# Low parts of some weight units made by GpSimd instead of VectorE, in a two-layer hybrid decoder on one Trainium2 core

## What is computed

```python
for l in range(DEPTH):                       # 2
    h = _rmsnorm(x, ln_g[l])                 # x: (1, 256, 2048) float32
    u = h @ w_in[l]                          # w_in: (2048, 6232)
    ...                                      # y_a GLA, y_b SSD, y_c MLA, y_d dilated attention
    y = jnp.concatenate([y_a, y_b, y_c, y_d], axis=-1)
    x = x + y @ w_out[l]                     # w_out: (2048, 2048)
```

## Time and profile before

| | us |
|---|---|
| median of 3 runs | 840.86 (840.15 to 841.04) |
| profiled execution | 841.09 |
| its span | 839.3 |
| PE busy | 833.8 |
| DVE busy | 525.9 |
| ACT busy | 475.0 |
| POOL busy | 47.1 |

### The profile page before, as it was taken

How to read it: one execution, slowest core, us unless ns; L and a number is a source line. 1 busy time by engine, 2 the same in 40 slices (tenths; PEclk the granted TensorE clock), 3 DMA queues, 4 the chain that set the end, 5 groups by cost and what they waited for, 6 DMA issues and landing times.

```text
span 839.3 us, 11336 instructions
## 1 busy us (share of the span) xinstructions
PE 833.8 (99%) x4350; PEld 703.4 (84%) x4350; DVE 525.9 (63%) x872; ACT 475.0 (57%) x788; POOL 47.1 (6%) x63
## 2 busy tenths in 40 slices
PE   9999999999999999999999999999999999999998
PEld 6888888997888888888888888889888888888886
DVE  6566764774886565644564577638749865556542
ACT  7666544776865566443546564456677565663441
POOL 7200000100200000000000000001002000000000
PEclk9999999999999999999999999999999999999999
DMA  9976652564654445656656666526546544546663
GB/s 342 336 252 215 210 174 82 170 169 131 182 174 150 151 134 167 200 186 193 205 191 189 187 217 193 176 82 192 143 124 202 169 148 128 176 132 215 195 188 123
DMA packets 46165, 150.97 MB, mean 180 GB/s; under 512 B 5344, under 2 KB 6032, under 8 KB 45600
## 3 DMA queue, kind: packets, MB, share of 16 engines
q1 hardware_dynamic: 45168, 147.62, 55.6%
q10 hardware_dynamic: 752, 2.57, 0.9%
q0 software_dynamic: 192, 0.07, 0.0%
HBM read 148.13 MB, written 2.11 MB: 179 GB/s over the span
## 4 chain that ended last, share of the span: by engine, by line
PE 97%; DVE 1%; ACT 1%; issue 0%; DMA 0%; ACTq 0%; DVEq 0%
PE gemm L637 28%; PE gemm L646 27%; PE gemm L638 27%; PE pairs L828 2%; PE pairs L714 1%; PE pairs L854 1%; PE pairs L843 1%; PE pairs L668 1%; PE pairs L835 1%; PE pairs L799 1%; PE pairs L568 1%; PE pairs L869 1%; DVE u L1483 0%; PE pairs L881 0%; PE pairs L882 0%; PE pairs L880 0%
## 5 line engine op out<-in xcount | busy, mean ns | idle before, releaser
L1359 DVE TENSOR_TENSOR w_lo<-raw,w_hi 128x1024 fp32r<-128x1024 f32 (+1 forms) x287 | 318.1, 1115 | 237.1 <-ACT w_hi L995 236.1
L637 PE MATMUL gemm<-w_hi,a_hi 128*128 128x512 f32 (+1 forms) x1144 | 425.2, 377 | 0.9 <-ACT w_hi L995 0.9
L638 PE MATMUL gemm<-w_hi,a_lo 128*128 128x512 f32 (+1 forms) x1144 | 414.3, 368 | 0.0
L995 ACT ACTIVATE w_hi<-raw 128x1024 fp32r<-128x1024 f32 (+1 forms) x287 | 273.9, 968 | 181.1 <-PE gemm L646 159.2
L646 PE MATMUL gemm<-w_lo,a_hi 128*128 128x512 f32 (+1 forms) x1144 | 281.4, 368 | 0.0
L637 PEld LDWEIGHTS gemm<-w_hi,a_hi 128*128 128x128 f32 x1144 | 215.1, 188 | 37.0 <-issue 2.6
L638 PEld LDWEIGHTS gemm<-w_hi,a_lo 128*128 128x128 f32 x1144 | 215.3, 188 | 33.6 <-issue 1.0
L646 PEld LDWEIGHTS gemm<-w_lo,a_hi 128*128 128x128 f32 x1144 | 203.6, 188 | 35.0
L1025 ACT ACTIVATE u<-gemm,st 128x512 f32<-128x512 f32 (+1 forms) x40 | 22.1, 604 | 15.9 <-PE gemm L646 15.9
L1209 ACT ACTIVATE arena<-arena,st 128x128 f32<-128x128 f32 (+1 forms) x32 | 13.1, 444 | 28.2 <-DVE st L1579 28.2
L542 POOL TENSOR_TENSOR st<-st,powers 128x4 f32<-128x4 f32 (+2 forms) x8 | 1.9, 240 | 446.6 <-ACT arena L1079 220.7
(11 more groups left out here) (197 smaller groups left out, 605.3 us busy)
## 6 DMA issues: line engine op xcount, KB each, us to landing
raw<-in_weights_dram SPq DMA_DIRECT2D x223, 512.0 KB, 3.6
raw<-in_weights_dram SPq DMA_DIRECT2D x64, 278.0 KB, 2.9
wuq<-in_w_uq_dram SPq DMA_DIRECT2D x2, 1152.0 KB, 6.1
x<-in_x_dram SPq DMA_DIRECT2D x4, 512.0 KB, 6.2
o<-ssd_rows ACTq DMA_DIRECT2D x2, 1024.0 KB, 6.6
param_rows<-in_params_dram SPq DMA_DIRECT2D x2, 904.0 KB, 7.6
u<-in_xT_dram SPq DMA_DIRECT2D x3, 512.0 KB, 8.1
out_dram<-x SPq DMA_DIRECT2D x3, 512.0 KB, 6.0
```

The lines of the kernel that those rows point to most:

```text
L637: pe.matmul(acc_t[t], a_hi[:, k, tok[t]], hi, start=k == 0, stop=False)
L638: pe.matmul(acc_t[t], a_lo[:, k, tok[t]], hi, start=False, stop=False)
L995: A_(w_hi[:, n % SPLIT, 0:c], raw[:, n % RAW, 0:c], ACT.Copy).then_inc(hi_done, 1)
L1359: TT(w_lo[:, n % SPLIT, 0:c], raw[:, n % RAW, 0:c], w_hi[:, n % SPLIT, 0:c].bitcast(F32), ALU.subtract).then_inc(split_done, 1)
```

## The change

From unit 12 of layer 0 on, and in all of layer 1, the low part of each unit with n % 4 == 3 is made by POOL, with the same subtraction on the same tiles; DVE skips these units. The one count `split_done` is replaced by two, `split["dve"]` and `split["pool"]`, and `split_of(l, n)` gives the count to wait for: how many units up to this one that engine has split. PE and SP wait for it; for its first four loads SP waits for nothing, and DVE no longer sets the count at the start. On POOL the eight reciprocal roots are placed between the subtractions by the table RSQRT_AT: a root stands behind the unit of its number, and behind that unit's subtraction if POOL has one there. It is 33 units in layer 0 and 36 in layer 1, 16 of them narrow.

```diff
--- before.py
+++ after.py
@@ -104,6 +104,10 @@
 WARM = 3
 
 GLA_AT = 26
+
+POOL_FROM = 12
+
+RSQRT_AT = {"x rs": 13, "gla rs": 47, "mla crs": 57, "mla rs 0": 74, "mla rs 1": 78, "dil rs 0": 81, "dil rs 1": 83, "ssd rs": 94}
 
 LEVELS = (64, 32, 16, 8, 4, 2, 1)
 NEG = -1e30
@@ -404,7 +408,8 @@
         row_out, row_in = sem("row_out"), sem("row_in")
         x_turned, x_hi, x_lo = sem("x_turned"), sem("x_hi"), sem("x_lo")
         weights_in = [sem(f"weights_in_{i}") for i in range(RAW)]
-        hi_done, split_done, unit_used = sem("hi_done"), sem("split_done"), sem("unit_used")
+        hi_done, unit_used = sem("hi_done"), sem("unit_used")
+        split = {"dve": sem("split_dve"), "pool": sem("split_pool")}
         stage = {e: sem(f"{e}_stages") for e in ORDER}
         setup = {e: sem(f"{e}_setup") for e in ORDER}
         seen = {e: [] for e in ORDER}
@@ -423,6 +428,15 @@
 
         def unit_width(n):
             return BLOCKS[n // UPB][2]
+
+        def splitter(l, n):
+
+            return "pool" if n % 4 == 3 and (l or n >= POOL_FROM) else "dve"
+
+        def split_of(l, n):
+
+            e = splitter(l, n)
+            return split[e], sum(splitter(*divmod(g, UNITS)) == e for g in range(l * UNITS + n + 1))
 
         def weights(l, n):
             return w_d[l, UNIT_AT[n]:UNIT_AT[n + 1]].rearrange("(p c) -> p c", p=P)
@@ -456,7 +470,8 @@
             for l in range(DEPTH):
                 for n in range(UNITS):
                     w = unit_width(n)
-                    sp.wait_ge(split_done, l * UNITS + n + 1)
+                    if l * UNITS + n >= RAW:
+                        sp.wait_ge(*split_of(*divmod(l * UNITS + n - RAW, UNITS)))
                     if (l, n) == (0, 0):
 
                         sp.dma_start(raw[:, 0, WB:2 * WB], weights(l, n)[:, WB:2 * WB]).then_inc(weights_in[0], 16)
@@ -547,14 +562,21 @@
 
                 pool.dma_start(w2[0:GLA_R, :], gla_w2[l]).then_inc(gate_in, 16)
                 pool.dma_start(w2[GLA_R:GLA_R + 1, :], gla_b[l].unsqueeze(0)).then_inc(gate_in, 16)
-                rsqrt("x rs", xrs, xss)
-                rsqrt("gla rs", grs, gss)
-                rsqrt("mla crs", crs, css)
-                rsqrt("mla rs 0", mrs[:, 0:8], mss[:, 0:8])
-                rsqrt("mla rs 1", mrs[:, 8:16], mss[:, 8:16])
-                rsqrt("dil rs 0", drs[:, 0:8], dss[:, 0:8])
-                rsqrt("dil rs 1", drs[:, 8:16], dss[:, 8:16])
-                rsqrt("ssd rs", brs, bss)
+                def lo(n):
+
+                    c = UK * unit_width(n)
+                    pool.wait_ge(hi_done, l * UNITS + n + 1)
+                    pool.tensor_tensor(w_lo[:, n % SPLIT, 0:c], raw[:, n % RAW, 0:c], w_hi[:, n % SPLIT, 0:c].bitcast(F32), ALU.subtract).then_inc(split["pool"], 1)
+
+                roots = {"x rs": (xrs, xss), "gla rs": (grs, gss), "mla crs": (crs, css), "mla rs 0": (mrs[:, 0:8], mss[:, 0:8]),
+                         "mla rs 1": (mrs[:, 8:16], mss[:, 8:16]), "dil rs 0": (drs[:, 0:8], dss[:, 0:8]),
+                         "dil rs 1": (drs[:, 8:16], dss[:, 8:16]), "ssd rs": (brs, bss)}
+                for n in range(UNITS):
+                    if splitter(l, n) == "pool":
+                        lo(n)
+                    for name, (dst, mean) in roots.items():
+                        if n == RSQRT_AT[name]:
+                            rsqrt(name, dst, mean)
 
                 pool.wait_ge(*reached("dve", l)("yT 3"))
 
@@ -600,7 +622,7 @@
                         pe.wait_ge(*dve(f"yT {(n - U_OUT) // 2}"))
                     if (l, n) == (DEPTH - 1, UNITS - 1):
 
-                        pe.wait_ge(split_done, l * UNITS + n + 1 + RAW)
+                        pe.wait_ge(*split_of(l, n))
                         for t in range(T):
                             acc_t, tok = acc_ps[:, b % 2, t, 0:w], slice(t * P, (t + 1) * P)
                             for j in range(UK):
@@ -623,7 +645,7 @@
                             for t in range(T):
                                 pe.matmul(acc_t[t], a_hi[:, k, tok[t]], hi, start=k == 0, stop=False)
                             if j:
-                                pe.wait_ge(split_done, 1 + RAW)
+                                pe.wait_ge(*split_of(0, 0))
                             else:
                                 pe.wait_ge(first_lo, 1)
                             pe.wait_ge(x_lo, j + 1)
@@ -1315,8 +1337,6 @@
         @block.vector
         def _(v):
             v.memset(A(0, WB), 0.0).then_inc(warm, 1)
-            v.sem_inc(split_done, RAW)
-
             v.wait_ge(cols_in, 16)
 
             def xT_lo(i, l):
@@ -1353,10 +1373,12 @@
                         xT_lo(0, 0)
                         xT_lo(1, 0)
                         v.wait_ge(hi_done, 1)
-                        TT(w_lo[:, 0, WB:c], raw[:, 0, WB:c], w_hi[:, 0, WB:c].bitcast(F32), ALU.subtract).then_inc(split_done, 1)
+                        TT(w_lo[:, 0, WB:c], raw[:, 0, WB:c], w_hi[:, 0, WB:c].bitcast(F32), ALU.subtract).then_inc(split["dve"], 1)
+                        return
+                    if splitter(l, n) == "pool":
                         return
                     v.wait_ge(hi_done, l * UNITS + n + 1)
-                    TT(w_lo[:, n % SPLIT, 0:c], raw[:, n % RAW, 0:c], w_hi[:, n % SPLIT, 0:c].bitcast(F32), ALU.subtract).then_inc(split_done, 1)
+                    TT(w_lo[:, n % SPLIT, 0:c], raw[:, n % RAW, 0:c], w_hi[:, n % SPLIT, 0:c].bitcast(F32), ALU.subtract).then_inc(split["dve"], 1)
 
                 def yT(j):
```

## The result

The changed kernel takes 842.35 us (median of 16 executions, 841.91 to 843.11), the kernel before 840.75 beside it. The ratio is 1.0019, 95% interval 1.0012 to 1.0027: 1.6 us slower, 1.0 to 2.3. It is a small loss, but the interval excludes no change. The profiled execution took 842.28 us, its span 840.4. POOL's subtraction is L569.

What follows compares the result with a forecast made beforehand. PE, busy 833.8 of 839.3 us, was taken as the bound, with at most 0.9 us to win. Layer 0's +0.6 and layer 1's +0.1 made +0.7 us: predicted median 841.5 us, range 840.1 to 843.4.

Steps and rivals of the forecast that it cites:

- The bound: Whole kernel: PE is busy 833.8 of 839.3 us, so the change can win at most 0.9 us.
- The price on POOL: POOL's subtractions, scaled from 0.60 us for 256 elements: 2.40 us for 1024 elements and 1.30 for 556.
- The lock: POOL and DVE block each other: POOL waits for DVE's running instruction, DVE's next waits for all of POOL's.
- The wide units: The 53 wide subtractions: about 8.9 us of slack for 2.4; tightest is unit 15 of layer 0. Cost 0.
- Step 1: Narrow stretch: POOL's subtraction for unit 51 blocks DVE's backlog, L1390 and the high part of 55 +0.5 us.
- Step 2: Unit 55's low part: POOL brings it 1.30 us behind the high part, PE wants it at 1.13: +0.15.
- Step 3, the loads: Unit 59's load goes some 1.1 us later, its high part comes 0.8 late, within cover: cost 0.
- Layer 1: Narrow stretch of layer 1: steps repeat at +0.6 us, idle time before unit 61 takes most: +0.1.
- the rival of blocking elsewhere: DVE's blocking reaches PE at attention steps or a root used by DVE: up to 1.2 us each, chance 0.05.
- The sum: Whole kernel: +0.6 us in layer 0 and +0.1 in layer 1 make +0.7, predicted median 841.5 us.
- Reciprocal roots between subtractions, the start, the end: POOL's eight roots queued between subtractions, SP's first four loads, and unit 143 of layer 1: cost 0 each.

Runs made afterwards that it cites:

- The best kernel here: Only the wide subtractions on POOL and ACT's silus one unit later, against the kernel before: 839.65 us, ratio 0.9988.

## Why the prediction was right or wrong, point by point

- **The bound: right.** PE's idle time between start and tail, 0.9 us, was taken as all that could be won. The best kernel here has none of it left and is 1.0 us faster (0.3 to 1.8).
- **The price on POOL: right for the wide ones, 7% low for the narrow.** 2.40 was forecast and 2.40 measured in most of the 53 (2469 ns in the mean, since some wait for DVE). For 556 elements I took 1.30 and it is 1.39 where nothing blocks it (unit 55). The two give (2.40 - 1.39)/468 = 2.2 ns an element and 0.2 us fixed, so neither strict proportion nor the 0.26 us row with its slope of 1.4 ns was right: the 0.60 that I read behind DVE's end already held little of the fixed part. The estimate from the figure of the Trainium skill, "GPSIMD Engine Reference", section "Performance versus the Vector engine" (2.25 and 1.22 us) was 6% and 12% low.
- **The lock: right.** A subtraction on POOL holds up DVE's two-operand instructions, and a memset doesn't.
- **The wide units: right.** No wait, ratio 0.9999 without the narrow ones. At unit 15 the cover left was to be 0.44 us and is 0.42 in the changed kernel.
- **Step 1: right in place and size.** +0.5 forecast, +0.47 and +0.41 measured. The idle time before unit 55 was to be 0.7 and is 0.64.
- **Step 2: right in place, too small.** +0.15 forecast, +0.44 in each layer. 0.09 is POOL's 1.39 for 1.30. For the rest the traces show two terms that the sum left out: PE's first matmul behind a wait is recorded at 0.39 us instead of 0.29, and POOL starts 0.08 us behind the end of the high part (164.73 to 164.81).
- **Step 3, the loads: right at a cost of 0, wrong in size.** No wait at 59 or 60. The high part of 59 was to be 0.8 us late. Against PE's schedule before the stretch it was 1.3 us late in layer 0 and 0.8 early in layer 1. Loads that nothing in the edit touches move as much (next point).
- **Layer 1: +0.1 forecast, +0.46 measured.** Unit 61 gave back 0.89 where I had 0.5. Missing was the low part of unit 62: I priced POOL's blocking where DVE's result reaches PE through ACT, and passed over a DVE w_lo with 0.54 us of cover right beside a subtraction on POOL. It was in the rival of blocking elsewhere, which named other places.
- **Unit 61's idle time hangs on the load of unit 59.** In layer 1 before, SP issues that load at 580.94 and ACT starts on it at 586.32, 5.4 us later. With unit 63 alone on POOL, where nothing of this layer differs up to there and the load is issued at the same point of PE's schedule, it is 581.63 and 585.86, 4.2 us, and PE isn't idle before unit 61. In both the chain from there (DVE's low part of 59, its last convolution step, ACT's silu, a table load) brings the high part of 61 some 4.6 to 4.7 us behind that of 59. These are ACT's rows with unit 63 alone and with the wide subtractions alone:

```profile
585.86 1.45 ACT L1017 ACTIVATE w_hi<-raw 128x556 fp32r<-128x556 f32 x2 [0.93 <-DMA raw<-in_weights_dram]
590.56 1.78 ACT L1017 ACTIVATE w_hi<-raw 128x556 fp32r<-128x556 f32 x3
...
585.59 1.40 ACT L1017 ACTIVATE w_hi<-raw 128x556 fp32r<-128x556 f32 x2 [1.27 <-DMA raw<-in_weights_dram]
590.24 1.79 ACT L1017 ACTIVATE w_hi<-raw 128x556 fp32r<-128x556 f32 x3
```

So these 0.6 us of idle time (0.9 by PE's schedule) come and go with the landing of one transfer, and that they are missing in a trace is by itself no gain of its edit. Why the transfer lands later in some executions is open. Whether it was PE's shift that used them up in the changed kernel, as the prediction has it, isn't shown either: there the high part of 59 came early as well.
- **The sum: the size was too small.** +0.7 forecast, +1.6 measured: 842.35 is inside the range of 840.1 to 843.4 and just above the 840.9 to 842.3 that I gave the best chance. The traces account for 1.16 to 1.37 of it. The terms that were too small are step 2 (0.6 us over both layers) and unit 62, which was put at nothing and costs 0.5. That the sum isn't further off is partly luck: unit 61 gave back 0.4 us more than I had, so 0.7 + 0.6 + 0.5 - 0.4 = 1.4.
- **Reciprocal roots between subtractions, the start, the end: right at 0.** No wait of PE names them.

## What to carry to other kernels

Work taken from an engine pays only if the busiest engine waits for it. Here DVE had 37% of idle time and was without a pause for some 11 us in the narrow stretch of a layer (150.96 to 162.39 in layer 0 before); helping it where it had slack did nothing, and where it was behind the helper took more of its time (about 1.1 us of blocking) than it gave (0.64 us). Before moving an elementwise step to GpSimd, price it from a row of the same kind, and then look at every two-operand DVE instruction that can fall beside it, above all at those whose result the bound engine wants within the length of the moved one. One-operand instructions aren't all safe: a TENSOR_SCALAR was held up too. When the bound engine idles behind a chain, look first at the order of the engine that hands the work on: moving two steps of ACT by one slot won what the helper could not.

## What the runs showed of the hardware

- POOL's TENSOR_TENSOR on fp32, written as fp32r: 2.40 us for 128x1024 and 1.39 for 128x556, 2.2 ns an element and 0.2 us fixed; DVE's takes 1.22 and 0.73.
- A DVE instruction with two SBUF operands that meets it is recorded longer by nearly all of POOL's run: 1.92 for 0.73, a step of 128x256 2.79 for four instead of 1.7. A DVE TENSOR_SCALAR of 128x256 with one tensor operand stretched too, 1.48 us for the 0.34 it takes alone. A TENSOR_TENSOR of 128x768 that reads one operand from PSUM (`pairs`) and one from SBUF did not: 0.95 us beside POOL's subtraction (586.68 with unit 59 alone on POOL), and 0.95 in the kernel before.
- POOL's memset of the same tile stretches neither.
- Whichever instruction starts first keeps the other out; 0.02 to 0.06 us decided over 0.5 us of PE's time.
- A load of 278 KB, that of unit 59 in layer 1, was taken up by ACT 5.4 us behind its issue in one execution and 4.2 in another, though nothing of that layer differs up to there.
